# The three value products of the merge in one-pass fp32r with split operands, and the second product moved behind its gates

## The reference

```python
o_a = mla_branch(...)      # 256 x 512, already multiplied by silu(gate)
o_b = fox_branch(...)
o_c = rwkv_branch(...)
g_a, g_b, g_c = jnp.split(merge_cols, 3, axis=-1)      # each 256 x 1024
merged = (jax.nn.sigmoid(g_a) * (o_a @ w_pa[l])
          + jax.nn.sigmoid(g_b) * (o_b @ w_pb[l])
          + jax.nn.sigmoid(g_c) * (o_c @ w_pc[l]))
x = x + (merged @ w_out[l])
```

## Time and profile before

| | |
|---|---|
| median of three runs | 1566.91 us (1564.62 to 1571.62) |
| the profiled execution: its time | 1561.43 us |
| its span in the profile | 1559.6 us |
| granted TensorE clock, mean | 0.992 |
| busy PE, DVE, ACT, POOL | 1473.2, 807.0, 560.3, 43.9 us |

### The profile page before, as it was taken

One profiled execution on the slowest core, in us unless ns is written; L12 is line 12 of the kernel. 1 busy time (PEld: TensorE's weight loads), 2 busy tenths in 40 slices (PEclk: granted clock), 3 DMA queues, 4 the chain that ended last, 5 costly groups with the idle time before them and its releaser, 6 DMA issues.

```text
span 1559.6 us, 21048 instructions
## 1 busy us (share of the span) xinstructions
PE 1473.2 (94%) x8918; PEld 1052.6 (67%) x8918; DVE 807.0 (52%) x1160; ACT 560.3 (36%) x856; POOL 43.9 (3%) x39
## 2 busy tenths in 40 slices
PE   6999999997999999998989999999999999999998
PEld 6876544543975444445887786888688786769876
DVE  4745122124554121126688664775577676647844
ACT  4541110112431101113564655433346538454422
POOL 0020000000020000000000000100000000001000
PEclk9999999998999999999999999999999999999999
DMA  8448999996569999992433344002454333240022
GB/s 363 162 181 344 422 422 422 422 422 250 191 236 376 423 422 423 423 422 116 153 130 122 126 145 154 36 2 78 143 190 177 111 121 136 105 165 1 2 108 81
DMA packets 47476, 340.26 MB, mean 218 GB/s; under 512 B 5296, under 2 KB 5296, under 8 KB 7568
## 3 DMA queue, kind: packets, MB, share of 16 engines
q1 hardware_dynamic: 45504, 328.03, 53.2%
q0 software_dynamic: 1872, 10.80, 1.8%
HBM read 337.76 MB, written 1.05 MB: 217 GB/s over the span
## 4 chain that ended last, share of the span: by engine, by line
PE 82%; DVE 10%; ACT 3%; DMA 3%; issue 2%; DVEq 0%; SPq 0%; ACTq 0%
PE bank L523 51%; PE bank L887 13%; PE bank L928 7%; PE bank L831 4%; PE bank L526 3%; DMA ring<-wfirst 2%; DVE d_lo L1804 2%; PE bank L860 1%; PE bank L865 1%; ACT arena L1370 1%; ACT d_hi L1409 1%; DMA ring<-wsecond 1%; DVE arena L2224 1%; DVE arena L1782 1%; PE bank L913 0%
## 5 line engine op out<-in xcount | busy, mean ns | idle before, releaser
L1804 DVE TENSOR_TENSOR d_lo<-ring,d_hi 128x2048 fp32r<-128x2048 f32 (+2 forms) x99 | 222.3, 2252 | 144.1 <-ACT d_hi L1409 143.8
L1409 ACT ACTIVATE d_hi<-ring 128x2048 fp32r<-128x2048 f32 (+2 forms) x103 | 193.2, 1882 | 142.5 <-PE bank L523 93.9
L523 PE MATMUL bank<-arena 128*128 128x128 f32 (+10 forms) x2016 | 218.4, 277 | 19.2 <-ACT arena L1370 5.9
L523 PEld LDWEIGHTS bank<-arena 128*128 128x128 f32 (+6 forms) x2016 | 188.3, 173 | 42.7 <-issue 21.0
L1370 ACT ACTIVATE arena<-bank 128x512 f32<-128x512 f32 (+3 forms) x222 | 125.1, 581 | 242.9 <-PE bank L523 163.2
L523 PE MATMUL bank<-xT_hi,d_hi 128*128 128x256 f32 x592 | 167.8, 283 | 3.0 <-ACT arena L1679 1.7
L523 PE MATMUL bank<-d_hi,xT_hi 128*128 128x512 f32 (+1 forms) x400 | 160.8, 402 | 8.0 <-DVE arena L2224 4.1
L523 PE MATMUL bank<-xT_hi,d_lo 128*128 128x256 f32 x592 | 166.7, 282 | 0.0
L523 PE MATMUL bank<-xT_lo,d_hi 128*128 128x256 f32 x592 | 166.2, 281 | 0.0
L523 PE MATMUL bank<-d_hi,xT_lo 128*128 128x512 f32 (+1 forms) x400 | 157.3, 393 | 0.0
L523 PE MATMUL bank<-d_lo,xT_hi 128*128 128x512 f32 (+1 forms) x400 | 156.5, 391 | 0.0
(11 more groups left out here) (336 smaller groups left out, 1874.9 us busy)
## 6 DMA issues: line engine op xcount, KB each, us to landing
ring<-wmoe SPq DMA_DIRECT2D x84, 1024.0 KB, 17.0
ring<-wsecond SPq DMA_DIRECT2D x80, 1024.0 KB, 4.6
arena<-wmoe SPq DMA_DIRECT2D x72, 1024.0 KB, 17.4
ring<-wfirst SPq DMA_DIRECT2D x30, 1024.0 KB, 4.6
wide<-wmoe SPq DMA_DIRECT2D x24, 1024.0 KB, 19.9
xT_raw<-wmoe SPq DMA_DIRECT2D x12, 1024.0 KB, 20.1
rows<-lnrows POOLq DMA_DIRECT2D x4, 1024.0 KB, 7.5
ring<-wsecond SPq DMA_DIRECT2D x4, 848.0 KB, 10.6
```

Of the source, the lines that this page charges most:

```text
L523: mark(nc.tensor.matmul(o, lhsT, rhs, start=start, stop=stop, skip_group_check=loose), full)
L1409: nc.scalar.activation(high_of(u)[:, 0:width], raw[u % NRAW][:, 0:width], ACT.Copy).then_inc(sem("piece_high"), 1)
L1804: v.tensor_tensor(d_lo[u % NRAW][:, 0:width], raw[u % NRAW][:, 0:width], high_of(u)[:, 0:width], SUB).then_inc(sem("piece_low"), 1)
```

## The change

The fourth entry of `pa`, `pb` and `pc` becomes True: their weights are split. The high part is made by ACT as for the others, the low part by POOL (`weight_low`). The left operands are split too. For `pa` and `pb` ACT copies `oT` (128 x 1024) into `oT_hi` and POOL subtracts into `oT_lo` (`o_high`, `o_low`). For `pc` ACT and DVE do it for each token tile (`y_high`, `y_low`). After `gated_out` and `gated_y` DVE copies one element to say that the output is there (`o_gated`). TensorE issues `three` where it issued `mm`. In layer order `pb` now stands behind `mg2` and `key_sums`, and the low parts of `mg3` stand on DVE behind `mixed_keys`.

```diff
-          ("v", ...), ("wa", ...), ("pa", 2, PROJ, False), ("mg0", ...), ("mg1", ...),
-          ("gc", 2, PROJ, True), ("pb", 2, PROJ, False), ("mg2", 2, PROJ, True), ("mg3", 2, PROJ, True),
-          ("mg4", ...), ("mg5", ...), ("pc", 2, PROJ, False), ("woa", ...), ("wob", ...)]
+          ("v", ...), ("wa", ...), ("pa", 2, PROJ, True), ("mg0", ...), ("mg1", ...),
+          ("gc", 2, PROJ, True), ("mg2", 2, PROJ, True), ("pb", 2, PROJ, True), ("mg3", 2, PROJ, True),
+          ("mg4", ...), ("mg5", ...), ("pc", 2, PROJ, True), ("woa", ...), ("wob", ...)]
...
+POOL_LOW += [PIECE_AT[f"{_name}.{_l}"] + _n for _l in range(DEPTH) for _name in ("pa", "pb", "pc") for _n in range(2)]
...
+            def merge_values(name, split):
+                pe_eng.wait_ge(sem("o_split"), split)
+                for b in range(4):
+                    pe_eng.wait_ge(bank_free[b], pe.used(b))
+                for n in range(2):
+                    w = [v3(half, 4) for half in piece(name, n)]
+                    for tt in range(TT):
+                        b, tok = n + 2 * tt, slice(tt * P, (tt + 1) * P)
+                        pe_eng.wait_ge(bank_free[b], pe.reuse(b))
+                        for k in range(4):
+                            three(banks[b][:, :], (oT_hi[:, k, tok], oT_lo[:, k, tok]), (w[0][:, k, :], w[1][:, k, :]),
+                                  k == 0, k == 3, full=b if k == 3 else None)
...
-                pe_eng.wait_ge(bank_free[4], pe.used(4))
-                merge_tiles(f"pc.{l}", oT_c)
+                merge_tiles(f"pc.{l}", l)          # tile tt waits for sem("o_split") >= 4 * l + tt + 3, then uses three()
...
                 low_rank(l, 1, (5, 6))
-                merge_values(f"pb.{l}", oT)
                 merge_gates(f"mg2.{l}")
                 key_sums(l, 1, 4)
+                merge_values(f"pb.{l}", 4 * l + 2)
                 merge_gates(f"mg3.{l}")
...
+            def o_high(n):                                              # ACT
+                act_eng.wait_ge(sem("o_gated"), n)
+                nc.scalar.activation(oT_hi, oT, ACT.Copy).then_inc(sem("o_high"), 1)
...
+                high_to(f"pa.{l}", 1)
                 turned_qk(FOXK)
                 ...
+                o_high(4 * l + 1)
+                high_to(f"pa.{l}", 2)
                 softmax()
...
+            def y_low(l, tt):                                           # DVE
+                tok = slice(tt * P, (tt + 1) * P)
+                dve_eng.wait_ge(sem("o_high"), 4 * l + tt + 3)
+                v.tensor_tensor(oc_lo[:, :, tok], oT_c[:, :, tok], oc_hi[:, :, tok], SUB).then_inc(sem("o_split"), 1)
...
+            def weight_low(at):                                         # POOL
+                u = POOL_LOW[at]
+                pool.wait_ge(sem("piece_high"), SPLITS[u] + 1)
+                nc.gpsimd.tensor_tensor(d_lo[u % NRAW][:, 0:HALF_SLOT], raw[u % NRAW][:, 0:HALF_SLOT], high_of(u)[:, 0:HALF_SLOT],
+                                        SUB).then_inc(sem("pool_low"), 1)
+            def o_low(n):
+                pool.wait_ge(sem("o_high"), n)
+                nc.gpsimd.tensor_tensor(oT_lo, oT, oT_hi, SUB).then_inc(sem("o_split"), 1)
```

More of the change, by code:

```diff
@@ L222, in two_blocks @@
         S_MARK = small[:, 600:604]
+        S_TOLD = small[:, 604:606]
         c1 = Carve()
@@ L671, in proj_tiles @@
                                   at == 0, at == KD - 1, full=b if at == KD - 1 else None)
[L673 to L683, removed]
             xT, memT = (xT_hi, xT_lo), (memT_hi, memT_lo)
@@ L1038, in apply, with merge_tiles @@
                     mm(o[:, P:T], vn[:, 1, h, :], PT[:, h % 2, T:T + P], start=False, full=ob if h % 2 else None, loose=True)
[L1040 to L1049, removed]
+            def merge_values(name, split):
+                pe_eng.wait_ge(sem("o_split"), split)
                 for b in range(4):
                     pe_eng.wait_ge(bank_free[b], pe.used(b))
+                for n in range(2):
[6 more added lines that the diff above has]
+                                  k == 0, k == 3, full=b if k == 3 else None)
+            def merge_tiles(name, l):
                 w = []
                 for tt in range(TT):
+                    tok = slice(tt * P, (tt + 1) * P)
+                    pe_eng.wait_ge(sem("o_split"), 4 * l + tt + 3)
                     for n in range(2):
@@ L1057, in merge_tiles @@
                         if tt == 0:
-                            w.append(v3(piece(name, n, n > 0), 4))
+                            w.append([v3(half, 4) for half in piece(name, n, n > 0)])
                         pe_eng.wait_ge(bank_free[b], pe.reuse(b))
@@ L1062, in merge_tiles @@
                         for k in range(4):
-                            mm(banks[b][:, :], oT[:, k, tt * P:(tt + 1) * P], w[n][:, k, :], start=k == 0, stop=k == 3, full=b if k == 3 else None)
+                            three(banks[b][:, :], (oc_hi[:, k, tok], oc_lo[:, k, tok]), (w[n][0][:, k, :], w[n][1][:, k, :]),
+                                  k == 0, k == 3, full=b if k == 3 else None)
             def low_rank(l, tt, bs):
@@ L1158, in _ @@
                 low_rank(l, 0, (5, 6))
-                merge_values(f"pa.{l}", oT)
+                merge_values(f"pa.{l}", 4 * l + 1)
                 merge_gates(f"mg0.{l}")
@@ L2246, in gated_out @@
                     v.tensor_tensor(oT[:, j, :], banks[j][:, 0:T], gates[:, g, j, :], MUL).then_inc(bank_free[j], dve.sends(bank_free[j]))
+                dve_eng.wait_ge(dve.last, dve.value)
+                v.tensor_copy(S_TOLD[:, 0:1], oT[:, 3, 0:1]).then_inc(sem("o_gated"), 1)
+            def y_low(l, tt):
+                tok = slice(tt * P, (tt + 1) * P)
+                dve_eng.wait_ge(sem("o_high"), 4 * l + tt + 3)
+                v.tensor_tensor(oc_lo[:, :, tok], oT_c[:, :, tok], oc_hi[:, :, tok], SUB).then_inc(sem("o_split"), 1)
             def gated_y(tt):
@@ L2252, in gated_y @@
                 v.tensor_tensor(oT_c[:, :, tok], v3(banks[4][:, :], 4), gates[:, 0, :, tok], MUL).then_inc(bank_free[4], dve.sends(bank_free[4]))
+                dve_eng.wait_ge(dve.last, dve.value)
+                v.tensor_copy(S_TOLD[:, 1:2], oT_c[:, 3, tok.start:tok.start + 1]).then_inc(sem("o_gated"), 1)
             def merge(s, first):
@@ L2552, in _ @@
                 mixed_keys(1)
+                low_to(f"mg3.{l}", 2)
                 merge(sgm, False)
@@ L2648, in _ @@
                 if n % 2:
-                    for u in POOL_LOW[n - 1:n + 1]:
-                        pool.wait_ge(sem("piece_high"), SPLITS[u] + 1)
-                        nc.gpsimd.tensor_tensor(d_lo[u % NRAW][:, 0:HALF_SLOT], raw[u % NRAW][:, 0:HALF_SLOT], high_of(u)[:, 0:HALF_SLOT],
-                                                SUB).then_inc(sem("pool_low"), 1)
+                    for at in range(n - 1, n + 1):
+                        weight_low(at)
                 if n:
@@ L2773 @@
         parts += pa + [c(c_mg), c(c_mg + 512), cT(c_gc)]
[L2774 removed]
+        parts += [c(c_mg + 1024)] + pb + [c(c_mg + 1536), c(c_mg + 2048), c(c_mg + 2560)] + pc + cut(a["w_out_2"][l], halves)
         second.append(cat(parts))
```

28 lines of the change are left out of this document (25 added, 3 removed).

## The result

The changed kernel took 1577.13 us (median of 7 runs, 1574.17 to 1580.04), the kernel before, in 7 runs beside it, 1566.91 (1564.62 to 1575.03): ratio 1.0063, 95% interval 1.0043 to 1.0083. It is slower by 10 us; 1577 was forecast. Measured once more beside other kernels it was 1577.57 against 1566.14 (1.0065, 1.0041 to 1.0089).

The account below looks back on a forecast made before the run. PE held 82% of the chain of waits, with DVE binding the first layer after `pa`. Terms 2.4 + 1.0 - 1.2 + 4.1 = +6.3, with the clock +10.3, gave a median of 1577 us, range 1561 to 1585.

Parts of the forecast that it names:

- PE's own saving: Six value products, each 48 fp32r matmuls, take 11.2 us instead of 13.81: 2.6 saved each, 15.8 us in all.
- The hold on `pa`: Before `pa`, DVE's small softmax tensor_scalar (L2232) waits for POOL's subtraction, 3.6 us later: +2.4 first layer, +1.0 second.
- a sign to look for: In the changed kernel's profile, PE idle about 4 us between `low_rank` and `pa`, in both layers.
- a chain over ACT and DVE: First layer around `pa`: ACT 3.6 us late, less 1.26 it idled before, gives +2.4, against +1.0 in the second.
- rival B: Ahead of `pa`, POOL does not block L2232, all else as forecast: 1567 to 1570 us; chance 0.26.
- `pb` behind `mg2`: PE waits 2.0 us before `mg2` for DVE's low part, later saves 2.6 on `pb`: -0.6 a layer, -1.2 in all.
- The key sum's copy: DVE's `key_sum` copy (L2290) moves into POOL's second low part: taken as 0, at most +1.5 us a layer if blocked.
- rival D: One-element DVE copies are blocked as well and each new idle drops the clock: +15.7, 1582 us; chance 0.15.
- `pc`: In the tail, `woa` 1 waits for `pc` 0's high slot, so `merge_last` comes 2.05 us later: +4.1 in all.
- The clock: Slow products after new PE idles before `pa` and the merged tiles: 2.5 drops of 1.6 us, +4, between 0 and 6.4.
- The total: Whole kernel: +6.3 us, with the clock +10.3; profiled execution 1571.7, median 1577 us.
- C: Operands come in time everywhere; PE's 15.8 us comes through but for the `mg2` seam (4.0): 1555 us; chance 0.17.

Follow-up runs that it names:

- a1_negate: Changed kernel with the softmax maxima taken by a negating reduction, so the small tensor_scalar is gone: 1568.15 us, ratio 1.0005 to the kernel before.
- b1_all: Changed kernel with five repairs (negating reduction, later POOL low part, earlier `mg2` low part, `pc` by column halves, `merge_last` ahead of `woa` 1's low part): 1552.16 us.
- b3_pc_tail: Changed kernel with `pc` column half by column half, and `merge_last` and two transposed low parts ahead of `woa` 1's low part on DVE: 1564.67 us, ratio 0.9986.
- c1_ones: Changed kernel with the softmax's 128x8 tensor_scalar issued as eight of 128x1: 1574.60 us, ratio 1.0042 to the kernel before.
- b2_hold: Kernel before, with only two unneeded POOL subtractions added in each layer: 1571.11 us, ratio 1.0022.
- a2_mg2_low: Changed kernel with DVE making the low part of `mg2`'s first piece ahead of `gated_out`: 1572.37 us, ratio 1.0042 to the kernel before.
- c3_all_again: Changed kernel with the five repairs of b1_all, measured once more: 1548.34 us, ratio 0.9877 to the kernel before.
- a4_fill: Changed kernel with dummy PE products in its new idles (before `pa`, before `mg2`, behind `pc`): 1579.18 us, ratio 1.0092 to the kernel before.

## Why the prediction was right

- **PE's own saving** (2.6 us a product). Right where the clock is full: `pa` took 11.27 to the next group's start in a1_negate's second layer and in b1_all (13.41 before, and 0.4 more in the group behind), `pc` 11.28 in b3_pc_tail (13.84 before). In the changed kernel the saving did not arrive in the total.
- **The hold on `pa`.** 3.6 us were forecast for L2232. In the second layer it lasted 3.29 (3.12 more), and PE's start came 3.6 later: right. In the first layer this was not what set PE's start, and that the size fits is luck. `pa` came 4.1 later there with no idle of PE before it, where 4 us were a sign to look for; the slow scores and `low_rank` set it, and the hold lay beside them (1.92 us, as the maxima came later). The 1.4 us that the first layer was to lose beyond the second, by a chain over ACT and DVE, are not seen: from `mg0` to `mg2` both lose 1.5. c1_ones and b2_hold show the cause of the hold from both sides.
- **A row misread.** The argument for rival B was that L1953 lost only 0.2 us beside POOL. But by the earlier trace rows that row began at 439.68, and POOL's subtraction ended at 440.07: it lost 0.2 because POOL was nearly done. It ended 0.15 to 0.16 us behind POOL's end in each of the 14 profiles of this case, so it was held as well. All 18 rows of L2248's kind and all 19 of two buffer inputs (128x512) that began inside a POOL subtraction ended within 0.6 us behind its end. Of 60 reductions and of 60 one-element copies and products inside one, none was stretched. So 0.26 for B was too much on the rows at hand. The rule of the Trainium skill ("SBUF — State Buffer", "Who interferes with whom") is borne out for the eight-element `tensor_scalar` by the rows of L2248; a one-element one was not held.
- **`pb` behind `mg2`.** The idle of 2.0 was 1.81. The term was -0.6 a layer and measures +0.9 (the rows of `mg0` to `mg3`): in this profile `mg2` lost 1.6 to the clock behind an idle for which the prediction had reserved no drop, in the second profile it did not. The cause of the idle was named only in part: behind DVE's low part stood bank 5 (a2_mg2_low).
- **The key sum's copy.** Not held: 0.15 us at 963.94, inside POOL's instruction, as one element is in c1_ones. So rival D's price for it was nothing here.
- **`pc`.** The idle was 4.48 (4.5 forecast), ACT's start and `merge_last` 1.93 later (2.05). The tail is +3.1 against the gates; the 1.1 beyond are the transposes at 1.2 GHz.
- **The clock.** This term was mis-sized: +4 in the sum. By the landmarks of the first profile it is 1.6 and 2.6 in the two `pa`, 1.6 in each `mg2`, 1.1 in each tail: 9.6. The 4.7 in the first layer's scores are not in it, as they stand in the place of the hold; the prediction had no slow products there, since it looked for them behind new idles of about 4 us only. The second profile has other places and about as long a time in both layers together (537.4 us from `v` to `woa`, 537.6 in the first), so the sum is better known than its parts.
- **The total.** The layers of the two traces differ by +15.6 where +10.3 was forecast. The medians differ by 10.2. That they met the forecast owes much to chance: the clock was 5.6 over its term, and the difference of the medians is 8.4 less than that of the two profiled executions, since that of before is a fast draw, 5.5 under its median, that of the changed kernel 2.9 above its own. The waits are shown, but for the first layer's `pa`; the agreement to 1 us is not a merit of the sum.

Rival B (no hold) and C (the saving comes through) fail by the rows above. What C supposed came about in b1_all and c3_all_again: 15 and 18 us under before, about the 15.8 of the products.

## What to carry to other kernels

Moving subtractions to an idle GpSimd is not free: in these traces the DVE instructions with two buffer inputs (128x512), and the `tensor_scalar` of 8 or 256 elements, that fell into one waited for its end. So look at what DVE has due at those times, and replace it (a negating reduction) or move POOL's instruction. Each new or longer idle of PE, here already of 1.6 us, is to be priced with the slow products that can follow it. Before a saving on PE is counted, ask who then ends PE's wait: here chiefly a negating reduction and the order of two loops and of two queues turned +10 us into -15 to -18. And where two delays lie beside each other, as the hold and the slow scores do, taking away one can show nothing.

## What was not expected of the hardware

- A `tensor_scalar` of 128x8 was held 3.1 us by POOL, eight of 128x1 together took 0.58 us in the same place.
- A PE idle of 1.3 to 1.8 us was followed by slow products in some executions and not in others: `mg2` to the next group took 13.3 us in one profile of the changed kernel and 11.7 in the other, behind the same idle of 1.81. What decides stays open.
- The 48 products of the scores and `low_rank` took 6.59 us, or else 11.0 to 12.5 at a lower clock. Without a4_fill, they were slow in 11 of 16 layers with an idle of 1.6 to 2.3 us before them (L2217 was held in all of them), and in 2 of 10 with 1.27. So the hold of L2217 makes them likelier, as far as these counts go. One of the two slow ones behind 1.27 makes the first layer's stretch to `pa` in the kernel with all repairs 30.1 us in one profile, where it is 26.7 in the other.
- The kernel before itself ranged from 1558 to 1576 us in these runs.
